# GpSimd's last pair of tables moved into a down-projection, and small fp32 matmul runs grouped

## The reference, cut to what matters

```python
for layer in range(DEPTH):
    h = h + 0.5 * swiglu(rmsnorm(h, norm_ff1[layer]), ff1_w_gate[layer], ff1_w_up[layer], ff1_w_down[layer])
    hn = rmsnorm(h, norm_mix[layer])
    mix = conv_ssm_mixer(hn, ...) if layer % 2 == 0 else window_attention(hn, ...)
    h = h + mix
    h = h + 0.5 * swiglu(rmsnorm(h, norm_ff2[layer]), ...)

def conv_ssm_mixer(hn, ...):
    xa, b_gate, c_gate, u = split(hn @ w_in)
    ya = b_gate * conv3(c_gate * xa)
    y = gelu(real(C @ scan(lam_bar, B_bar @ u)) + d_skip * u)     # 32 groups of 16 channels, 64 states
    yb = y * sigmoid(y @ glu_w + glu_b)
    return concat(ya, yb) @ w_out
```

## Time and profile before

| | us |
|---|---|
| median of 3 executions | 1913.57 |
| lowest and highest | 1913.55, 1915.07 |
| the profiled execution | 1914.02 |
| its span, first to last instruction | 1912.2 |

### The profile page before, as it was taken

The page is one execution under the profiler, slowest core; times in us unless marked ns, Lnnn a source line. Parts: engine busy times, 40 slices in busy tenths (PEclk is TensorE's granted clock), DMA queues, the critical chain, the costliest instruction groups (busy, mean ns, idle before and its releaser), DMA issues.

```text
span 1912.2 us, 33816 instructions
## 1 busy us (share of the span) xinstructions
PE 1898.7 (99%) x13887; PEld 1792.1 (94%) x13887; DVE 958.2 (50%) x1077; ACT 598.7 (31%) x707; POOL 349.8 (18%) x629
## 2 busy tenths in 40 slices
PE   8999999999999999999999999999999999999999
PEld 8999999999999999999999999999988778888887
DVE  5444356568765443344554433445557654434443
ACT  5222222332243222222342222223455432222222
POOL 2888789315230000000000000000011000000000
PEclk9999999999999999999999999999999999999999
DMA  6322444547523332432243323322321233233322
GB/s 180 89 82 83 143 141 126 160 132 187 122 70 87 92 88 83 110 88 71 70 123 88 82 83 99 88 80 77 113 62 45 67 88 99 82 97 99 107 69 85
DMA packets 330785, 188.29 MB, mean 98 GB/s; under 512 B 8152, under 2 KB 323832, under 8 KB 330712
## 3 DMA queue, kind: packets, MB, share of 16 engines
q1 hardware_dynamic: 323296, 166.81, 31.4%
q0 software_dynamic: 7088, 20.38, 4.0%
q10 hardware_dynamic: 328, 0.07, 0.0%
HBM read 174.91 MB, written 11.14 MB: 97 GB/s over the span
## 4 chain that ended last, share of the span: by engine, by line
PE 97%; DVE 2%; ACT 1%; issue 0%; ACTq 0%; DVEq 0%
PE ps L793 79%; PE ps L1009 5%; PE ps L1120 2%; PE ps L1051 2%; PE ps L1070 1%; PE ps L1252 1%; PE ps L1217 1%; PE ps L1161 1%; PE ps L1186 0%; PE ps L1172 0%; PE ps L1182 0%; PE ps L970 0%; PE ps L969 0%; PE ps L960 0%; PE ps L838 0%
## 5 line engine op out<-in xcount | busy, mean ns | idle before, releaser
L793 PE MATMUL ps<-xl,wh 128*128 128x264 f32 (+1 forms) x2432 | 563.8, 301 | 0.0
L793 PE MATMUL ps<-xh,wh 128*128 128x264 f32 (+1 forms) x2432 | 562.6, 301 | 0.8 <-DVE t_a L1601 0.7
L793 PE MATMUL ps<-xh,wl 128*128 128x264 f32 (+1 forms) x2432 | 562.4, 301 | 0.0
L1548 DVE TENSOR_TENSOR wl<-raw,wh 128x2048 fp32r<-128x2048 f32 x171 | 399.9, 2338 | 172.1 <-ACT wh L1263 172.1
L1263 ACT ACTIVATE wh<-raw 128x2048 fp32r<-128x2048 f32 x172 | 327.7, 1905 | 253.0 <-PE ps L793 211.2
L793 PEld LDWEIGHTS ps<-xh,wh 128*128 128x128 f32 x2432 | 389.9, 188 | 17.8 <-DVE t_a L1601 0.9
L793 PEld LDWEIGHTS ps<-xl,wh 128*128 128x128 f32 x2432 | 388.8, 188 | 15.6 <-issue 0.2
L793 PEld LDWEIGHTS ps<-xh,wl 128*128 128x128 f32 x2432 | 388.6, 188 | 14.9
L793 PE MATMUL ps<-act_l,wh 128*128 128x264 f32 (+1 forms) x1232 | 284.7, 301 | 0.0
L793 PE MATMUL ps<-act_h,wh 128*128 128x264 f32 (+1 forms) x1232 | 284.7, 301 | 0.0
L793 PE MATMUL ps<-act_h,wl 128*128 128x264 f32 (+1 forms) x1232 | 284.3, 301 | 0.0
(11 more groups left out here) (308 smaller groups left out, 1724.4 us busy)
## 6 DMA issues: line engine op xcount, KB each, us to landing
raw<-in_ff_w_gate SPq DMA_DIRECT2D x88, 512.0 KB, 4.0
raw<-in_ff_w_up SPq DMA_DIRECT2D x87, 512.0 KB, 5.2
raw<-in_ff_w_down SPq DMA_DIRECT2D x64, 384.0 KB, 4.1
raw<-in_ff_w_down SPq DMA_DIRECT2D x64, 320.0 KB, 3.7
raw<-in_even_w_in SPq DMA_DIRECT2D x16, 512.0 KB, 5.3
raw<-in_attn_w_qkv SPq DMA_DIRECT2D x12, 512.0 KB, 4.3
raw<-in_even_w_out SPq DMA_DIRECT2D x8, 512.0 KB, 4.5
raw<-in_attn_w_o SPq DMA_DIRECT2D x8, 512.0 KB, 4.6
```

The lines of the kernel that those rows point to most:

```text
L793: last = nc.tensor.matmul(ps[:, 2 * pair + hf, 0:nh], w[:, slot, b * P:(b + 1) * P], x[:, k0 + k, c0 + hf * nh:c0 + (hf + 1) * nh], start= ...
L1548: v.tensor_tensor(wl[:, c % 2, :], raw[:, c % 2, :], wh[:, c % 2, :].bitcast(F32), ALU.subtract).then_inc(wl_ready, 1)
```

## The change

In GpSimd's loop over channel tiles a wait is added ahead of the last tile's two tables: they start when the first down tile of the second part of the first SwiGLU is evacuated. In the mixer, the kernel runs of tiles 1 to 3 move from their own places to right behind the output runs of tiles 0 to 2, and the state runs of tiles 1 to 3 from the tile's start that followed to right behind the feature runs of tiles 0 to 2. VectorE's `kernel_evac(1)` to `kernel_evac(3)` move behind `evac(5)`, `evac(8)` and `evac(11)`. `XN` and `YN`, the counts of the waits, are made from `STAGES` and follow.

```diff
-        STAGES = {6: "k0", 8: "s0", 10: "k1", 12: "o0", 13: "y0", 14: "s1", 16: "k2",
-                  18: "o1", 19: "y1", 20: "s2", 22: "k3", 24: "o2", 25: "y2", 26: "s3", 29: "o3", 31: "y3"}
+        STAGES = {6: "k0", 8: "s0", 12: "o0 k1", 13: "y0 s1", 18: "o1 k2", 19: "y1 s2", 24: "o2 k3", 25: "y2 s3", 29: "o3", 31: "y3"}
@@ GpSimd
             for ft in range(KC):
+                if ft == KC - 1:
+                    pool.wait_ge(tile_evac, FF[0][1] + 2 * NF + KD + 1)
                 table(ft, c4, 2, c2, 1, 0, T + 1, 0)
                 input_table(ft)
@@ VectorE
             split_mix(3)
-            kernel_evac(1)
             input_tables(1)
             conv_gate(0)
             evac(5)
+            kernel_evac(1)
             split_mix(4)
...
             evac(7)
-            kernel_evac(2)
             input_tables(2)
             split_mix(5)
             conv(1)
             evac(8)
+            kernel_evac(2)
             y_low(1)
...
             split_mix(6)
-            kernel_evac(3)
             input_tables(3)
             evac(11)
+            kernel_evac(3)
             conv(2)
```

## The result

The kernel after takes **1921.05 us** (median of seven executions, 1920.39 to 1922.88), the kernel before on the same chip 1914.39 us (1913.55 to 1916.87). The ratio is 1.0035, interval 1.0026 to 1.0044: slower, by 6.7 us. The profiled execution took 1922.88 us, its span is 1920.8 us.

A forecast was written before the change was run, and what follows sets the result against it. The prediction took TensorE, busy 99% of the span, to bound the kernel. Its terms, -0.9 + 4.7 + 1.3 - 0.3 + 0.4 + 0.6 = +5.8 us, on a median of 1913.57 gave 1919.4 us, range 1913.4 to 1921.8.

The forecast's parts named there:

- The stall at 336, -0.9: TensorE's wait at 336 us beside GpSimd's table products goes, as those products leave that place: -0.9 us.
- The turns, +4.7: Second part's down-projection: `ssq`, `xl` and the split each wait for a GpSimd product, delaying TensorE's third down tile: +4.7 us.
- one turn less: Lower case for the down-projection loss: product 1 starts after the addition to `ssq`, costing 2.8 us.
- The bound for a single turn: Lower case for the down-projection loss: only the split waits, for one product, 2.5 - 0.8 = 1.7 us.
- The second round, +0.5: Next down-projection round: five input-table products put off `ssq`, `xl` and split by about 2 us, losing 0.5 us more.
- The clock: After TensorE's gap in the down-projection the clock falls to half speed: +1.3 us, 0.5 us of it the second round's.
- The loads, nothing: GpSimd's mixer loads, queued behind the moved tables, come 31 us later but have 33 us of cover: no cost.
- The fp32 runs, -0.3: Mixer: six changes between fp32 and fp32r runs go, at 0.05 us each: -0.3 us, bounds -1.2 and 0.
- y1, +0.4: Mixer: y1 waits for VectorE's copies of k2, which stand behind evacuation 8: +0.4 us, 0 to 0.7.
- o3, +0.6: Mixer: o3 waits for `states(3)`, whose end moves by 2.0 us against 1.35 us of slack: +0.6 us, 0 to 1.

The follow-up runs named there:

- one-turn run: Kernel before, last tile's first 1152-wide product let go behind the second round's addition to `ssq`, the other seven each in a hole behind a later split: 1913.99 us.
- the later start: Kernel before with only GpSimd's new wait, released by the second addition to `ssq` in place of the first down tile's evacuation: 1917.79 us, ratio 1.0016.
- run with halves: Kernel before with only GpSimd's new wait, the last tile's 1152-wide products and 1024-wide subtraction each cut in two: 1916.13 us, ratio 1.0010.
- run with k3 back: Kernel after with the fourth kernel run (k3) put back ahead of the third output step (o2): 1920.45 us, one time.
- the wait alone: Kernel before with only GpSimd's new wait for the first down tile ahead of the last tile's tables, mixer as before: 1921.19 us, ratio 1.0032.
- no last tables: Kernel before, GpSimd leaving out the eight products of the last channel tile's two tables, so its results are wrong: 1915.14 us, ratio 1.0000.
- paced: Kernel before, each of the last tile's eight table products waiting for its own count of finished weight splits (30 to 33): 1914.85 us, ratio 1.0001.
- writes only: Kernel before with only GpSimd's new wait, each last-tile product replaced by two memsets of its output, so its tables are zeros: 1915.21 us, ratio 1.0001.
- one turn at the split: Kernel before, last tile's first product let go by the event that starts the split, the other seven in holes behind later splits: 1915.18 us, ratio 1.0002.
- the regrouping alone: Kernel before with only the mixer's regrouped fp32 runs and moved VectorE copies, without GpSimd's new wait: 1915.06 us, ratio 1.0001.

## Why the prediction was right

The forecast was 1919.4 us and slower; 1921.05 is inside the range. Of the 1.65 us between them 0.8 is the starting point, as before took 1914.39 beside it and not 1913.57; the change was forecast at +5.8 and is +6.7 in the medians. The mechanism was forecast and found; that the trace's own sum, +5.7, is so near is in part luck, since errors cancel in it. By its steps, on the trace after:

- **The stall at 336, -0.9**: -0.90. The pair is in time there.
- **The turns, +4.7**: 4.44. Forecast on the clock of before: `ssq` from 358.22 to 360.5, `xl` to 363.5, the split 366.0 to 368.3. Measured, less 0.55: to 360.3, 363.0 and 367.7. Three turns, each a little shorter than 2.3 to 2.5 us. The step had two errors that cancel, which is luck: the products were shorter, and the slack was not 0.8 us. In the trace after the pair starts 0.47 us behind the end of the split (368.23 to 368.70), in the one-turn run 0.49 us (364.15 to 364.64). So of the 0.77 us from the split's end to TensorE's start in the earlier trace rows only 0.3 us is slack. The one-turn run fits: 1.12 - 0.3 = 0.8 us.
- **The bounds.** The 2.8 us given to "one turn less" is the later start's wait to the digit, by the same two errors. The bound for a single turn was 1.7 us; with the rest of one product it was 0.8. The Trainium skill ("SBUF — State Buffer", section "SBUF: two separate sides") has the pair of ports held for a whole instruction; the trace agrees, with a split of 4.71 us where it is 2.29 us alone. Which of the two is served next it doesn't state; the runs show that each VectorE operation behind the other loses a turn of its own.
- **The second round, +0.5**: 0 in the trace after. Its operations are stretched (1.19, 1.56, 3.15 us), and its split ends at 372.26 + 3.15 = 375.41. The forecast said that the round begins late too; against TensorE it begins early. The evacuation at 368.15 comes 0.55 us ahead of the third tile's start at 368.70, where in the earlier trace rows it comes 0.32 us behind (364.03 and 363.71): 0.87 us more for the round. At full clock the fourth tile would be due 7.32 us after the third, at 376.02, and 375.41 + 0.48 is just in time. The half clock, which puts the tile off by 1.6 us more, was not needed for it. It hid something in the run with the later start: there the third tile starts at 365.49 and the second split ends at 373.16, which at full clock would have cost 0.8 us. The run with halves, where the clock does not fall, has a second gap of 1.0 us.
- **The clock**: 1.62, its bound of 1.6. The 1.3 us of the forecast held the second round's 0.5 us too, so the two together were forecast at 6.0 us with the turns, and measured at 6.06.
- **The loads, nothing**: 0.12 us in after, 0.9 in the run with k3 back. I had looked at who waits for the loads, and not at what they run beside.
- **The fp32 runs, -0.3**: 0. Fences of before and after, the runs with the pairs behind them:

```profile
502.20 0.66 PE L978 MATMUL ps<-ident,arena 66*128 66x66 f32 x8
...
502.99 0.40 PE L1009 MATMUL ps<-xl,wh 128*128 128x264 f32 x2
...
505.67 1.90 PE L960 MATMUL ps<-arena 128*128 128x66 f32 x16
...
507.70 0.40 PE L1009 MATMUL ps<-xl,wh 128*128 128x264 f32 x2
```

```profile
509.11 0.66 PE L979 MATMUL ps<-ident,arena 66*128 66x66 f32 x8
509.61 1.95 PE L961 MATMUL ps<-arena 128*128 128x66 f32 x16
...
511.69 0.40 PE L1010 MATMUL ps<-xl,wh 128*128 128x264 f32 x2
```

  Apart they take 0.79 + 2.03 us to the second pair behind them, of which one pair spacing each, 0.245, is other work: 2.33 us. Joined, 2.58 - 0.245 = 2.33 us. With the kernel run it is the same: 0.91 us from its start to the second pair in the earlier trace rows, and 0.91 us behind the output run after, with the same 0.08 us at its entry.
- **y1, +0.4**: 0. The addition behind k2's copies ends at 484.66, y1 starts at 484.92, when it is due. **o3, +0.6**: 0.25. `states(3)` came 1.5 us later and not 2.0: evacuation 12 starts at 514.68 (505.87 in before, and TensorE is 6.91 us behind at y2), so it was put off by 1.9 us and not by 2.4. The other 0.16 us of the mixer lies at no wait: against before s0 starts 6.74 us behind, y0 6.79, y1 6.85 and y2 6.91. Why is open.

The trace's own sum is +5.7 us, the difference of the medians 6.7. Stretches at half clock outside the change could make up the last microsecond, and the profiled execution has 3 us of them; how much of it they are in the median was not measured.

## What to carry to other kernels

VectorE with two SBUF operands and GpSimd's products take turns by whole instructions, so a move of one engine's work is costed per operation of the other that meets it, each with up to one full turn, against the slack of that very round. Slack is not counted up to the consumer's start: behind the split TensorE needed 0.47 to 0.49 us, behind `states(3)` 0.10 us (523.29 to 523.39 in after), so it is read at a place where the consumer really waits. If such work has to go beside a tight loop, start each piece behind the loop's longest operation, or cut the pieces small: halves brought the 6.9 us of the wait alone down to 2.0 (medians against before). And what follows the moved work moves as well: its loads then compete with another stage's weights.

## What the runs showed of the hardware

- **The clock after gaps.** Behind the gaps of 4.4, 4.2 and 2.9 us the granted clock was 0.57 to 0.63 over four microseconds: half speed for 3.4 us, 1.6 us lost. Behind the single gap of 0.8 us, the two of 0.9 us and the one of 1.05 us at 398 us TensorE's pairs kept their 0.245 us. Here no run had a gap in between.
- **The clock without a gap.** In some executions it falls in the attention stage, at 1406 to 1414 us, beside work that looks alike in both (windows of after, then of before):

```profile
1410.00:1414.00 4.00, 4.00 (x30) 3.57 (x30) 1.79 (x6) 3.96 (x5) 0.41 (x2) 1.00 0.05 13
1414.00:1418.00 4.00, 4.00 (x12) 3.16 (x11) 0.89 (x2) 1.52 (x3) 2.87 (x14) 0.57 0.01 2
```

```profile
1406.00:1410.00 4.00, 4.00 (x19) 3.24 (x19) 1.69 (x3) 2.40 (x3) 2.65 (x12) 1.00 0.01 2
```

  It costs 1.5 us. Near the start the half clock of the earlier trace rows lasts 3.4 us in some executions and 6.8 in others. The mean granted clock of the span tells the two kinds apart: 46 of 74 executions of the kernel before have 0.999, but only 12 of 42 of the four kernels that lose nothing or little at 336 and in the down-projection (no last tables, paced, writes only, one turn at the split). Among executions with 0.999 those four take 1912.8 to 1913.3 us (medians) and before 1913.9 to 1914.0: in executions at full clock the gain of 0.6 to 1.2 us is there, and it is not in the medians over all, since fewer of the executions are at full clock. The other kernels do not make a rule of it: 8 of 10 for the one turn behind `ssq`, 5 of 11 for the regrouping alone, 4 of 10 for the halves. What sends an execution one way or the other was not found out.
- **Who is first.** Of two operations let go at almost the same time either can hold up the other for its whole length: with the same release `xl` took 2.85 us in one kernel, where the records begin 0.01 us apart, and 0.77 us in another, where `xl` began 0.08 us ahead.
- **A change between fp32 and fp32r** showed as 0.08 us at the entry of a kernel run and as nothing ahead of o and y, and joining two short runs gave nothing back.
